# Page gathers spread between rotations, bias sums and a memory copy issued earlier, and a decoder's attention items in another order

## The chip, the cores and the metric

The kernel runs on one core of a Trainium2 chip, in float32. The metric is the device time of one execution in microseconds. Three runs of the kernel before gave 590.39, 592.55 and 594.27 us; the median is 592.55 us.

## The reference, cut to what matters

One layer of a hybrid decoder runs over 512 prompt tokens and over 8 decoding sequences of 4 tokens each, the latter with 1024 past positions in pages of 128. All projections come from one product x @ w_in. The change touches the decoding part (`mla_attend`, `nsa_attend`) and the compression of keys (`compress`):

```python
def compress(kv, w):
    bias = w['cmp_b1'] + jnp.einsum('pkd,kpde->ke', w['cmp_pos_emb'], w1)
    hid = bias[None, None, :, None, :]
    for r in range(ratio):
        proj = jnp.einsum('bcpkgd,kpde->bckge', ch, w1c[:, r])
        hid = hid + proj[:, r:r + nc]
    return jnp.einsum('bckge,ked->bckgd', jax.nn.silu(hid), w['cmp_w2'])

def mla_attend(q_lat, q_rope, q_pos, kv_row, k_pos):
    s = jnp.einsum('bthc,bkc->bhtk', q_lat, ckv) + jnp.einsum('bthr,bkr->bhtk', q_rope, krope)
    p = masked_softmax(s.astype(jnp.float32) * MLA_SCALE, k_pos[None, :] <= q_pos[:, None])
    return jnp.einsum('bhtk,bkc->bthc', p.astype(ckv.dtype), ckv)

def nsa_attend(q, q_rot, q_pos, gates, kv_c, cmp_end, imp_map, gather_sel, win_kv, win_pos):
...
    o = g[:, :, 0] * o_cmp + g[:, :, 1] * o_sel + g[:, :, 2] * o_win
```

Of the three branches of `nsa_attend`, `o_cmp` reads the compressed blocks, whose weights choose the blocks that `o_sel` reads; `o_win` reads the last 512 positions. The updated window buffer `s_win` is one of the outputs: the old buffer moved on by 4 tokens, with the new rows behind.

## The kernel before, in words

`plan()` (L183) writes one list of steps; every engine walks the same list and does its own part of each step, so an engine's order is the list's order. Semaphores join the engines. SP issues all big transfers in an order written out by hand (L713 to L831), with a wait before each that says which buffer has come free.

The stages, in the order of time: the six column blocks of w_in are multiplied one after the other (`proj` steps, blocks B_MLA, B_Q, B_CMPSEL, B_WINGATE, B_ZNSA, B_ZMLA, each for four prompt tiles and the 32 decoding tokens). POOL rotates queries and keys (`rope`, L1911) when ACT has copied a product out; two products later PE transposes the result (`post`). Woven into these, the compressed keys are made: `bias` (L1748 on VectorE: the sum of the position embeddings times cmp_w1, in two products and two reductions, then a small matmul and an addition), then `hid`, `hexp`, `hsilu`, `cmpout` for four groups of past pages and, last, for the prompt (`chunks`). Then come the prompt's attention units (`pscore`, `pnorm`, `pturn`, `pvalue`, numbered 0 to 51), and woven into units 18 to 35 the decoding part; at the end the output product with w_o and the layer norm.

Rotary keys of the past are fetched by 16 indirect DMAs that POOL issues one behind the other in `gather_krope` (L1969), at the step `("hid", 2, 0)`.

Decoding goes by six items (ITEMS, L164): latent attention, selected blocks and sliding window, each for two groups of four sequences. An item is `score` (matmul against the pages in SBUF), `min`, `exp`, `norm`, `probs` (transposes), `pv` (matmul against the pages' values), and for some `oturn`. Pages lie in seven slots of 8 KB per partition (0 to 4 in `ring`, 5 and 6 in `wring`, 7 in `w1h`). LOADS (L356) says for each block of pages its slot and whose `pv` must have ended before SP may load it. A latent or selected block is one sequence's 8 pages, fetched by 8 DMAs whose addresses are page numbers; SP first reads these from `ptab` into registers, 32 of them for four sequences (`numbers`, L670). A block of the window covers two sequences, takes 2 DMAs and needs no page numbers.

The diff touches the functions printed here.

Of the kernel before, what the change touches and what calls it, by code (L numbers as in the profile page):

```python
# [42 lines left out]
GB = 4  # L43
# [120 lines left out]
ITEMS = [("mla", 0), ("mla", 1), ("sel", 0), ("win", 0), ("sel", 1), ("win", 1)]  # L164
# [18 lines left out]
def plan():  # L183
# [21 lines left out]
    for now, _ in products[:first]:  # L205
        steps += now

    cmp = [([("bias",)], .5)]
    for n, t in enumerate(CMP_ORDER):
# [3 lines left out]
        if n == 2:  # L213
# [3 lines left out]
                chunks(1, 1)]  # L217
    cmp.append(([("cmpout", CMP_ORDER[-1])], 1))
    gates = len(products) - 2 * PT - 1
    steps += weave(products[first:gates], cmp + [([], 6)])  # L220
# [30 lines left out]
    for n, x in enumerate(ITEMS):  # L251
# [5 lines left out]
        if last and last[0] != "sel":  # L257
            body.insert(3, ([("oturn", "sel" if last[0] == "win" else "mla", last[1])], 1))
        g = {("mla", 1): 0, ("win", 0): 1}.get(x)
# [3 lines left out]
        if x == ("sel", 0):  # L263
# [61 lines left out]
def o_uses(kind, *a):  # L325
    if kind == "pvalue":
        i, unit, x = UNITS[a[0]]
        return int(spare_bank(i, unit) and x == 0)
    return int(kind in ("cmpout", "zpre") or (kind == "pv" and a[0] != "win"))
# [9 lines left out]
def build(nc, io):  # L339
# [34 lines left out]
    with ExitStack() as ctx:  # L374
# [108 lines left out]
        olatT = take(SR)  # L483
        qm = take(H * QH)
# [36 lines left out]
        impr, impm, dropb = take(SEL_TILES), take(SEL_TILES), take(SEL_TILES)  # L521
# [27 lines left out]
        sel_read = sem("sel_read")  # L549
# [106 lines left out]
        def _(sp):  # L656
# [39 lines left out]
            def load_slot(what, k, after, held=None):  # L696
# [7 lines left out]
                elif after and after[0] == "sel":  # L704
                    sp.wait_ge(sel_read, after[1] + 1)
                elif after:
                    wait_full(sp, O, O.at("pv", *(("sel", after[1]) if after[0] == "win" else after)))
# [57 lines left out]

            sp.wait_ge(gate_done, NT)
# [8 lines left out]

            held = [numbers(b) for b in range(GB)]
            for t in range(NT):
# [32 lines left out]
            wait_full(sp, O, O.at("pv", "sel", NG - 1))  # L810
# [22 lines left out]
        def _(pe):  # L833
# [211 lines left out]
            def weigh(kind, g):  # L1045
# [4 lines left out]
                u = O.at("pv", "sel" if kind == "win" else kind, g)  # L1050
                out = bank_of(O, u) if kind == "win" else claim(O, u)
# [5 lines left out]
                pe.matmul(out[:, 0:P], PTs[0:NS_TOK, pages, :], new, start=(kind != "win"), stop=False)  # L1057
                if kind == "sel":

                    for b in range(GB):  # L1060
                        pe.matmul(out[b * RB:(b + 1) * RB, 0:P], PcT[:, 1, b * RB:(b + 1) * RB],
                                  vc[:, g * GB + b, :], start=False, stop=False)

                for k in range(pages):
                    for b in range(GB):
                        last = k == pages - 1
# [1028 lines left out]
```

## Time and profile before

| | |
|---|---|
| median of three runs | 592.55 us |
| profiled execution | 591.65 us |
| its span, first to last instruction | 589.7 us |
| busy: PE / DVE / ACT / POOL | 491.9 / 258.0 / 153.6 / 135.1 us |
| granted TensorE clock, mean | 0.911 |

The profiled execution is 1.95 us longer than its span. Busy PE time includes matmuls whose ends are modelled, and it is longer where the granted clock is at the lower of its two levels (0.5, which is 1.2 GHz, against 1.0, which is 2.4 GHz).

### The profile page before, as it was taken

The page shows a single profiled execution, that of the slowest core. Times are in us where ns is not written, and L with a number is a line of the kernel's source. Part 1 is how long each engine was busy: PE and PEld are TensorE (multiplying, and loading weights), DVE is VectorE, ACT ScalarE, POOL GpSimd, SP SyncE. Part 2 cuts the span into 40 slices and gives each one's busy share as a digit, 9 for nine tenths or more (in the row PEclk, how much of TensorE's full clock was granted, in tenths as well). Part 3 has the DMA queues.
Part 4 walks back from the last instruction along what each step waited for, and adds up shares of the span by engine and source line. Part 5 has one row for each costly group of instructions (what it writes and reads, how often), then busy time and mean ns, then how long its engine had stood idle before and what let it go on. Part 6 is the DMA issues. An engine that isn't in the chain of part 4 may idle for free. (4 is left out here: it accounts for less than half of the span.)

```text
span 589.7 us, 8838 instructions
## 1 busy us (share of the span) xinstructions
PE 491.9 (83%) x2940; PEld 285.0 (48%) x2940; DVE 258.0 (44%) x673; ACT 153.6 (26%) x431; POOL 135.1 (23%) x222
## 2 busy tenths in 40 slices
PE   6969949999449999799969738468889998999894
PEld 3434436647338554444644525244545665554341
DVE  0041151330302557776966535355425755344415
ACT  0070001211001303433522423133254534233000
POOL 0033532235452111322222111011033432311000
PEclk9979969999859899899959979699889997999898
DMA  8974402442611905000132375864006201002101
GB/s 281 288 246 142 144 1 88 134 144 74 196 53 38 351 6 144 1 2 1 36 110 90 101 252 219 293 190 170 1 1 238 93 1 46 1 1 72 71 0 72
DMA packets 49159, 64.72 MB, mean 110 GB/s; under 512 B 10362, under 2 KB 39546, under 8 KB 49018
## 3 DMA queue, kind: packets, MB, share of 16 engines
q1 hardware_dynamic: 48218, 63.10, 32.3%
q0 software_dynamic: 512, 1.05, 0.7%
q8 instruction: 23, 0.38, 0.3%
q14 instruction: 22, 0.18, 0.1%
q10 hardware_dynamic: 384, 0.01, 0.0%
HBM read 59.89 MB, written 8.41 MB: 116 GB/s over the span
## 5 line engine op out<-in xcount | busy, mean ns | idle before, releaser
L1417 ACT ACTIVATE wring<-wring,small 128x128 f32<-128x128 f32 (+3 forms) x96 | 53.3, 555 | 111.1 <-DVE small L1604 110.6
L888 PE MATMUL psum<-wring,bufA 128*128 128x512 f32 (+1 forms) x192 | 73.6, 538 | 0.0
L1604 DVE CUSTOM_DVE_ANT_0 wring<-psum,const 128x128 f32<-128x128 f32 (+3 forms) x96 | 43.4, 483 | 40.6 <-PE psum L1098 30.8
L870 PE MATMUL psum<-bufA,wring 128*128 128x512 f32 x128 | 60.2, 621 | 0.1
L1314 PE MATMUL psum<-ring,zsil 128*128 128x512 f32 x128 | 58.2, 612 | 0.0
L1950 POOL TENSOR_SCALAR wring<-wring,small,gate 128x128 f32<-128x128 f32 (+3 forms) x32 | 24.3, 760 | 125.6 <-DVE small L1722 124.8
L888 PEld LDWEIGHTS psum<-wring,bufA 128*128 128x128 f32 x192 | 36.7, 194 | 31.4 <-issue 28.4
L843 PE MATMUL psum<-const,wring 128*128 128x128 f32 x248 | 38.7, 287 | 2.4 <-ACT mid L1425 2.4
L843 PEld LDWEIGHTS psum<-const,wring 128*128 128x128 f32 x248 | 28.6, 145 | 22.7 <-issue 17.3
L1314 PEld LDWEIGHTS psum<-ring,zsil 128*128 128x128 f32 x128 | 24.4, 195 | 29.8 <-issue 29.8
L870 PEld LDWEIGHTS psum<-bufA,wring 128*128 128x128 f32 x128 | 24.5, 198 | 28.3 <-issue 28.2
L963 PE MATMUL psum<-ring,w1h 128*128 128x256 f32 x128 | 33.8, 424 | 0.3 <-DVE small L1764 0.3
L1783 DVE RECIPROCAL rtmp<-rtmp 128x512 f32<-128x512 f32 (+1 forms) x10 | 33.5, 3350 | 0.3
L1947 POOL TENSOR_SCALAR wring<-wring,small 128x512 f32<-128x512 f32 (+3 forms) x16 | 19.0, 1187 | 60.4 <-DVE small L1722 60.2
L854 PE MATMUL psum<-wring,bufA 128*128 128x416 f32 x64 | 27.3, 575 | 4.6 <-DMA wring<-in_w_in 4.6
L963 PEld LDWEIGHTS psum<-ring,w1h 128*128 128x128 f32 x128 | 26.9, 215 | 5.4 <-issue 0.7
L843 PE MATMUL psum<-const,bufA 128*128 128x128 f32 (+4 forms) x90 | 15.6, 307 | 15.9 <-ACT mid L1425 7.6
L1966 POOL TENSOR_TENSOR zsil<-zsil,rtmp 128x512 f32<-128x512 f32 (+1 forms) x10 | 12.7, 1265 | 70.3 <-DVE rtmp L1783 70.3
L1014 PE MATMUL psum<-ring,bufA 128*32 128x512 f32 x56 | 15.2, 889 | 16.0 <-DMA ring<-in_sel_pages 8.6
L1144 PE MATMUL psum<-mid,kv 128*64 128x128 f32 x320 | 25.0, 287 | 2.4 <-ACT mid L1425 2.3
L1888 DVE SCALAR_TENSOR_TENSOR bufA<-bufA,psum 128x512 f32<-128x512 f32 x8 | 5.5, 687 | 43.5 <-PE psum L1314 43.5
L1095 PE MATMUL psum<-wring,ring 96*128 96x512 f32 (+3 forms) x64 | 22.0, 468 | 0.2 <-DVE ring L1855 0.2
(234 smaller groups left out, 725.1 us busy)
## 6 DMA issues: line engine op xcount, KB each, us to landing
ring<-in_cmp_pages SPq DMA_DIRECT2D x64, 128.0 KB, 2.3
wring<-in_w_in SPq DMA_DIRECT2D x3, 2048.0 KB, 9.0
ring<-in_sel_pages SPq DMA_DIRECT2D x48, 128.0 KB, 2.3
ring<-in_mla_pages SPq DMA_DIRECT2D x40, 128.0 KB, 2.9
ring<-in_w_om SPq DMA_DIRECT2D x1, 4096.0 KB, 14.2
out_s_win<-in_state_win_kv SPq DMA_DIRECT2D x1, 4064.0 KB
ring<-in_win_pages SPq DMA_DIRECT2D x6, 512.0 KB, 5.8
bufA<-in_x_t SPq DMA_DIRECT2D x8, 272.0 KB, 5.0
```

The costliest lines, as they stand in the source:

```text
L843: return pe.transpose(out, in_, ident[0:in_.shape[0], 0:in_.shape[0]])
L854: ins = pe.matmul(bank[:, 0:w], xT[:, c, t * P:(t + 1) * P], wr[:, 0, c, 0:w], start=(c == 0), stop=(c == KC - 1))
L870: ins = pe.matmul(bank, wr[:, b % 2, k, c * P:(c + 1) * P], xT[:, k, 0:SEQ], start=(k == 0), stop=(k == KC - 1))
L888: ins = pe.matmul(bank[:, 0:w], xT[:, c, t * P:(t + 1) * P], wr[:, b % 2, c, 0:w], start=(c == 0), stop=(c == KC - 1))
L963: ins = pe.matmul(out, w1[:, k, c, :, :].rearrange("p r e -> p (r e)"), chunks, start=(c == 0), stop=(c == 7))
L1095: ins = pe.matmul(bank[:, 0:keys], QT[:, i % 2, h, :], KT[:, h, 0:keys], start=True, stop=True)
L1144: ins = pe.matmul(bank[g * HD:(g + 1) * HD, x * P:(x + 1) * P], v, PTp[:, n % 2, at:at + P], start=(kind == "pmla" and x == 0 and j == 0), ...
L1314: ins = pe.matmul(bank, zT[:, c, ORDER[n] * P:(ORDER[n] + 1) * P], wo[:, c, half * 512:(half + 1) * 512], start=(c == 0), stop=(c == KC - 1))
L1417: ins = act.activation(p, p, ACT.Exp, bias=nmp[:, n % 4, g:g + 1], scale=-1.0, accum_out=lp[:, n % 4, g:g + 1])
L1604: dve.tensor_tensor_reduce(out, src, mask, -scale, CLAMP, ALU.add, ALU.min, least).then_inc(pool.free[u % pool.n], 1)
L1783: dve.reciprocal(e, e).then_inc(z_recip, 1)
L1950: ins = pool.tensor_scalar(p, p, c, gate3[:, i, at:at + 1], ALU.mult, ALU.mult)
```

## The change

Six things are edited.

- The 16 gathers become 16 steps `("krope", at)`. Four stand in each group of compression steps from the second on, between the products; each issues one gather.
- The sums of the bias become a step `bsum` of their own, which stands behind the seventh product (between the first and the second tile of B_Q). The step `bias` keeps the matmul and the addition.
- ITEMS puts both window items before the selected ones. The compressed values now go into the window's product, `pv` of the window and of the selected item have a PSUM use each, and VectorE keeps the window's rows in `orow_win` and adds the selected ones to them. The mask `dropb` is kept per group. The four `vup` steps come earlier, `kup` stays with the last item.
- LOADS is rewritten: the window's four blocks wait for the first latent item and take slots 2, 3, 0, 4; the first group's selected blocks wait for the second latent item (slots 5, 6, 1, 7); the second group's wait for the window items (slots 2, 3, 0, 4).
- On SP, the DRAM copy of the window buffer is issued before the gates' rows. Directly behind the last latent blocks now stand the window loads, the first group's page numbers, its selected blocks, the second group's page numbers and its selected blocks; the 25 stores of new rows, which stood ahead of the selected loads, stand behind all of them.
- `qlat` on PE waits for the copy `qhT` alone (`qh_turned`) instead of the whole `qhead` step; the first latent score waits for that.

```diff
-ITEMS = [("mla", 0), ("mla", 1), ("sel", 0), ("win", 0), ("sel", 1), ("win", 1)]
+ITEMS = [("mla", 0), ("mla", 1), ("win", 0), ("win", 1), ("sel", 0), ("sel", 1)]
...
+    products[NT + 1:NT + 1] = [([("bsum",)], 0)]
...
+        if n:
+            for j in range(4):
+                cmp.insert(len(cmp) - 8 + 2 * j, ([("krope", 4 * (n - 1) + j)], 0))
...
-        g = {("mla", 1): 0, ("win", 0): 1}.get(x)
+        g = {("mla", 1): 0, ("win", 1): 1}.get(x)
...
-        if x == ("sel", 1):
+        if x == ("win", 1):
             body += [([("vup", t)], .9) for t in range(PT)]
...
-             (("sel", 0, 0), 4, ("mla", 0)), (("sel", 0, 1), 2, ("mla", 0)), (("sel", 0, 2), 3, ("mla", 0)),
-             (("sel", 0, 3), 0, ("mla", 0)), (("win", 0, 0), 1, ("mla", 1)), (("win", 0, 1), 7, ("mla", 1)),
-             (("sel", 1, 0), 5, ("mla", 1)), (("sel", 1, 1), 6, ("mla", 1)), (("sel", 1, 2), 4, ("sel", 0)),
-             (("sel", 1, 3), 2, ("sel", 0)), (("win", 1, 0), 3, ("sel", 0)), (("win", 1, 1), 0, ("sel", 0))]
+             (("win", 0, 0), 2, ("mla", 0)), (("win", 0, 1), 3, ("mla", 0)), (("win", 1, 0), 0, ("mla", 0)),
+             (("win", 1, 1), 4, ("mla", 0)), (("sel", 0, 0), 5, ("mla", 1)), (("sel", 0, 1), 6, ("mla", 1)),
+             (("sel", 0, 2), 1, ("mla", 1)), (("sel", 0, 3), 7, ("mla", 1)), (("sel", 1, 0), 2, ("win", 0)),
+             (("sel", 1, 1), 3, ("win", 0)), (("sel", 1, 2), 0, ("win", 1)), (("sel", 1, 3), 4, ("win", 1))]
...
+            sp.dma_start(io["s_win"][0, :, 0:WIN - DEC_T].rearrange("b t k g d -> b (t k g d)"),
+                         io["state_win_kv"][0, :, DEC_T:].rearrange("b t k g d -> b (t k g d)")).then_inc(win_copy, 16)
             sp.wait_ge(gate_done, NT)
...
+            for x in LOADS[8:12]:
+                load_slot(*x)
             held = [numbers(b) for b in range(GB)]
+            for x in LOADS[12:16]:
+                load_slot(*x, held)
+            held = [numbers(GB + b) for b in range(GB)]
+            for x in LOADS[16:]:
+                load_slot(*x, held)
             for t in range(NT):
...
-            for x in LOADS[8:12]:
-                load_slot(*x, held)
-            sp.dma_start(io["s_win"][0, :, 0:WIN - DEC_T].rearrange("b t k g d -> b (t k g d)"),
-                         io["state_win_kv"][0, :, DEC_T:].rearrange("b t k g d -> b (t k g d)")).then_inc(win_copy, 16)
-            held = [numbers(GB + b) for b in range(GB)]
-            for x in LOADS[12:]:
-                load_slot(*x, held)
...
-                if kind == "sel":
+                if kind == "win":

                     for b in range(GB):
...
-                    wait_copied(pe, T, T.at("qhead"))
+                    pe.wait_ge(qh_turned, 1)
                     u = A.at("qlat")
...
+                        wait_copied(pe, T, T.at("qhead"))
-                    if step == ("score", "sel", 0):
+                    if step == ("score", "win", 0):
                         pe.wait_ge(bd_ready, 1)
...
-                if kind == "bias":
+                if kind == "bsum":
                     dve.wait_ge(pos_in, 16)
                     dve.wait_ge(wsmall_in, 16 * 10)
...
                     ins.then_inc(bias_sum, 1)
+                elif kind == "bias":
                     dve.wait_ge(const_in, 16)
...
-                    ok(dve.memset(qbd, 0.0))
-                    dve.tensor_copy(qhT, bank[0:NOPE, :])
+                    dve.memset(qbd, 0.0)
+                    dve.tensor_copy(qhT, bank[0:NOPE, :]).then_inc(qh_turned, 1)
+                    dve.wait_ge(qh_turned, 1)
...
-                    u = O.at("pv", "sel", a[1])
-                    dve.tensor_copy(orow, arrive(O, u)[:, 0:P]).then_inc(O.free[u % O.n], 1)
+                    u = O.at(*step)
+                    dve.tensor_copy(orow_win[:, a[1], :], arrive(O, u)[:, 0:P]).then_inc(O.free[u % O.n], 1)
+                elif kind == "pv" and a[0] == "sel":
+                    u = O.at(*step)
+                    dve.tensor_tensor(orow, arrive(O, u)[:, 0:P], orow_win[:, a[1], :], ALU.add).then_inc(
+                        O.free[u % O.n], 1)
...
-            def gather_krope():
-
-                pool.wait_ge(rope_pages_in, 16 * DEC_B)
...
+            def gather_krope(at):
+
+                if at == 0:
+                    pool.wait_ge(rope_pages_in, 16 * DEC_B)
...
+                g, k = divmod(at, PAGES)
+                pool.indirect_dma_start(
+                    out=krp[:, g, k * P:(k + 1) * P], out_offset=None,
+                    in_=io["krope_pages"].rearrange("n r p -> (n r) p"),
+                    in_offset=bass.IndirectOffsetOnAxis(ap=ropeidx[:, at:at + 1], axis=0)).then_inc(k_land[g], 16)
...
-                if step == ("hid", CMP_ORDER[2], 0):
-                    gather_krope()
+                if step[0] == "krope":
+                    gather_krope(step[1])
```

## Rows read from the trace of the kernel before

**Rows 1.** The waits: engine, line, releaser, us in total, times, longest.
```profile
PE psum L843 <- POOL kv L1925: 16.8, 1, 16.8
...
PE psum L1167 <- DVE mid L1758: 8.3, 1, 8.3
```

**Rows 2.** The timeline (start, length, engine, line, operation): the bias sums and `hid`.
```profile
75.54 2.15 DVE L1755 TENSOR_TENSOR mid<-w1h,mid 128x512 f32<-128x512 f32 x2
...
80.98 1.87 DVE L1758 TENSOR_REDUCE mid<-mid 128x64 f32<-128x1024 f32 x1
...
83.86 6.35 PE L963 MATMUL psum<-ring,w1h 128*128 128x256 f32 x16 [0.31 <-DVE small L1764]
...
103.97 3.72 PE L963 MATMUL psum<-ring,w1h 128*128 128x256 f32 x16
```

**Rows 3.** The timeline of DVE between the first and second tile of B_Q.
```profile
51.37 0.29 DVE L1549 COPY krT<-psum 32x128 f32<-32x128 f32 x1
...
58.28 0.19 DVE L1549 COPY krT<-psum 32x32 f32<-32x32 f32 x1
```

**Rows 4.** The timeline around the gathers.
```profile
146.11 7.71 PE L888 MATMUL psum<-wring,bufA 128*128 128x280 f32 x32
...
150.35 0.20 ACT L1395 ACTIVATE gate<-psum 128x24 f32<-128x24 f32 x1
...
154.41 0.95 POOL L1980 DMA_INDIRECT mid<-in_krope_pages,ropeidx  x1 [5.88 <-issue]
...
168.91 0.32 POOL L1920 TENSOR_TENSOR rtmp<-kv,const 128x64 f32<-128x64 f32 x1
...
170.65 0.69 PE L843 MATMUL psum<-const,kv 128*128 128x128 f32 x2 [16.83 <-POOL kv L1925]
...
171.13 5.31 PE L963 MATMUL psum<-ring,w1h 128*128 128x256 f32 x16
```

**Rows 5.** Windows: busy us (instructions) of PE, PEld, DVE, ACT, POOL; clock, DMA share, GB/s.
```profile
164.10:166.20 2.10, 0.00 (x0) 0.00 (x0) 0.00 (x0) 0.00 (x0) 0.01 (x1) 0.50 0.12 31
...
304.00:308.00 4.00, 4.00 (x22) 2.26 (x23) 2.61 (x10) 2.51 (x6) 0.00 (x0) 0.50 0.01 2
```

**Rows 6.** The timeline around the latent queries.
```profile
298.41 0.42 DVE L1791 COPY bufA<-psum 64x256 f32<-64x256 f32 x1
...
300.73 2.98 PE L1191 MATMUL psum<-bufA,w1h 64*128 64x32 f32 x13 [3.67 <-DVE bufA L1798]
```

**Rows 7.** The timeline of SP's issues; a merged row reaches from its first to its last.
```profile
291.43 8.07 SPq L693 DMA_DIRECT2D wring<-in_mla_pages  x16
...
332.27 16.73 SPq L693 DMA_DIRECT2D ring<-in_sel_pages  x32
349.05 0.83 SPq L800 DMA_DIRECT2D out_s_win<-in_state_win_kv  x1
368.36 0.83 SPq L711 DMA_DIRECT2D ring<-in_win_pages  x2
```

**Rows 8.** Transfers: times issued, KB each, median us from issue to landing.
```profile
ring<-in_sel_pages SPq DMA_DIRECT2D x48, 128.0 KB, 2.3
...
ring<-in_win_pages SPq DMA_DIRECT2D x6, 512.0 KB, 5.8
```

**Rows 9.** The timeline of PE in the decoding stage.
```profile
351.62 3.64 PE L1014 MATMUL psum<-ring,bufA 128*32 128x512 f32 x16 [8.64 <-DMA ring<-in_sel_pages]
...
378.05 1.07 PE L1014 MATMUL psum<-ring,bufA 128*32 128x512 f32 x2 [7.34 <-issue]
...
396.70 1.07 PE L1014 MATMUL psum<-wring,bufA 128*32 128x512 f32 x2 [0.76 <-DMA ring<-in_sel_pages]
...
400.41 2.22 PE L1098 MATMUL psum<-selKT,qrT 64*128 64x512 f32 x4
...
416.64 1.13 PE L1098 MATMUL psum<-winKT,qrT 64*128 64x512 f32 x4
...
445.50 1.08 PE L1067 MATMUL psum<-ring,w1h 128*32 128x128 f32 x32
```

More of the change, by code:

```diff
@@ L204, in plan @@
     first = NT + 3
-    for now, _ in products[:first]:
+    products[NT + 1:NT + 1] = [([("bsum",)], 0)]
+    for now, _ in products[:first + 1]:
         steps += now
@@ L217, in plan @@
                 chunks(1, 1)]
+        if n:
+            for j in range(4):
+                cmp.insert(len(cmp) - 8 + 2 * j, ([("krope", 4 * (n - 1) + j)], 0))
     cmp.append(([("cmpout", CMP_ORDER[-1])], 1))
     gates = len(products) - 2 * PT - 1
-    steps += weave(products[first:gates], cmp + [([], 6)])
+    steps += weave(products[first + 1:gates], cmp + [([], 6)])
     def slot(m):
@@ L256, in plan @@
         body += [([("exp", *x)], 1.5), ([("norm", *x)], 1.5)]
-        if last and last[0] != "sel":
-            body.insert(3, ([("oturn", "sel" if last[0] == "win" else "mla", last[1])], 1))
-        g = {("mla", 1): 0, ("win", 0): 1}.get(x)
+        if last and last[0] != "win":
+            body.insert(3, ([("oturn", *last)], 1))
+        g = {("mla", 1): 0, ("win", 1): 1}.get(x)
         if g is not None:
@@ L328, in o_uses @@
         return int(spare_bank(i, unit) and x == 0)
-    return int(kind in ("cmpout", "zpre") or (kind == "pv" and a[0] != "win"))
+    return int(kind in ("cmpout", "zpre", "pv"))
 def v_uses(kind, *a):
@@ L483, in build @@
         olatT = take(SR)
+        orow_win = qrope.rearrange("p (g n) -> p g n", g=NG)
         qm = take(H * QH)
@@ L520, in build @@
         grow = take(6).rearrange("p (b g) -> p b g", b=3)
-        impr, impm, dropb = take(SEL_TILES), take(SEL_TILES), take(SEL_TILES)
+        impr, impm = take(SEL_TILES), take(SEL_TILES)
+        dropb = [take(SEL_TILES) for _ in range(NG)]
         selc = take(2)
@@ L703, in load_slot @@
                     wait_full(sp, A, A.at("proj", after[1], NT - 1))
-                elif after and after[0] == "sel":
-                    sp.wait_ge(sel_read, after[1] + 1)
                 elif after:
-                    wait_full(sp, O, O.at("pv", *(("sel", after[1]) if after[0] == "win" else after)))
+                    wait_full(sp, O, O.at("pv", *after))
                 kind, g, b = what
@@ L1049, in weigh @@
                     wait_copied(pe, T, T.at("probs", kind, g, j // 2, j=j % 2))
-                u = O.at("pv", "sel" if kind == "win" else kind, g)
-                out = bank_of(O, u) if kind == "win" else claim(O, u)
+                u = O.at("pv", kind, g)
+                out = claim(O, u)[:, 0:P]
                 if kind == "mla":
@@ L1056, in weigh @@
                     new = kv3[0:NS_TOK, ST, col + G * HD:col + KVW]
-                pe.matmul(out[:, 0:P], PTs[0:NS_TOK, pages, :], new, start=(kind != "win"), stop=False)
-                if kind == "sel":
+                pe.matmul(out, PTs[0:NS_TOK, pages, :], new, start=True, stop=False)
+                if kind == "win":
                     for b in range(GB):
-                        pe.matmul(out[b * RB:(b + 1) * RB, 0:P], PcT[:, 1, b * RB:(b + 1) * RB],
-                                  vc[:, g * GB + b, :], start=False, stop=False)
+                        pe.matmul(out[b * RB:(b + 1) * RB, :], PcT[:, 1, b * RB:(b + 1) * RB], vc[:, g * GB + b, :],
+                                  start=False, stop=False)
                 for k in range(pages):
                     for b in range(GB):
-                        last = k == pages - 1
-                        ins = pe.matmul(out[b * RB:(b + 1) * RB, 0:P], PTs[:, k, b * RB:(b + 1) * RB],
-                                        pages_of(kind, g, b)[:, k, P:2 * P], start=False, stop=last and kind != "sel")
-                ins.then_inc(sel_read if kind == "sel" else O.full[u % O.n], 1)
+                        ins = pe.matmul(out[b * RB:(b + 1) * RB, :], PTs[:, k, b * RB:(b + 1) * RB],
+                                        pages_of(kind, g, b)[:, k, P:2 * P], start=False, stop=(k == pages - 1))
+                ins.then_inc(O.full[u % O.n], 1)
             def scores(n):
@@ L1669, in nsa_out, with drop_block @@
                 ins.then_inc(T.free[u % T.n], 1)
-            def drop_block():
+            def drop_block(g):
                 mids = slice(1, SEL_TILES - 2)
@@ L1807, in _ @@
                 elif kind == "norm":
-                    if step == ("norm", "sel", 0):
+                    if step == ("norm", "win", 0):
                         dve.wait_ge(grow_in, 16)
@@ L1843, in _ @@
                     wait_copied(dve, A, A.at("imp1", a[0]))
-                    drop_block()
+                    drop_block(a[0])
                 elif kind == "onsa":
```

27 lines of the change are left out of this document (10 added, 17 removed).

## The prediction

> **What bounds the kernel now.** I read the waits first, then the timeline around the longest of them, then the queue of SP. PE is busy for most of the span, and its busy stretches follow one another by the list of steps; so a wait of PE that goes away brings everything behind it forward, until another wait takes its place. Five waits are touched. PE waits 16.8 us for a rotation on POOL and 8.3 us for the bias sums [rows 1]; 3.67 us for the latent queries [rows 6]; 8.64 and 7.34 us for pages in the decoding stage [rows 9]. The first three are waits for an engine's order. The last two are waits for SP: it is one queue, and in it a page number costs time before any transfer is issued.
>
> **Bias sums.** DVE begins them at 75.54 and ends at 82.85, 7.3 us [rows 2]. PE has nothing else by its list, starts `hid` at 83.86 and needs 6.27 us for it (the next product begins at 90.13), where the same work takes 3.72 at 103.97 [rows 2]: the granted clock had fallen to its lower level behind the wait. In the new place DVE has ended its evictions at 51.66 and is idle until PE's next transposes, some 6.3 us later; the sums would last until 59.0, and the last of three small evictions behind them (0.5 us together) until 59.5, where it ended at 58.47 before [rows 3]. PE's next transposes claim that PSUM bank: 1.0 us lost. At `bias` a small matmul and an addition remain, some 1.4 us: `hid` runs from 76.9 to 80.6 instead of to 90.1. **Gain 9.5 us**, lost cover counted. If POOL's rotations beside the sums slow them by as much as those of rows 2 differ (2.15 against less), it is 8.5; nothing here makes it more than 10.5.
>
> **Gathers.** All 16 stand on POOL ahead of the rotation of the second-last B_CMPSEL product and of all of B_WINGATE. PE ends the second B_WINGATE product at 153.82 and resumes at 170.65; `hid` then takes 5.14 us at the lower clock [rows 4] instead of 3.72 [rows 2]. With the gathers spread, that rotation can begin when ACT has ended at 150.55 and takes 1.7 us (from 168.91 to 170.6) [rows 4]: ready at 152.3, 1.5 us before PE wants it. The next has two gathers ahead of it, 2 x 1.25 us (0.95 and the 0.30 between two), and PE wants it only after a `hid` and a product, 8 us later. `hid` would end at 153.82 + 0.45 + 3.72 = 158.0 instead of at 176.3. **Gain 18.3 us.** Below: one gather waited 5.88 us [rows 4]; if one does so again ahead of a rotation, up to 5 us are lost. Above: nothing, the wait can't be less than none. What is late next? By the list, two `hid`, two products and their transposes stand between (an estimate of 14 us) until the compressed rows that return from DRAM are wanted, and SP's issue of them moves by the 9.5 us of the first term; I estimate 7 us of slack, and more than 20 for the z weights, the next load.
>
> There is a rule against this part. In the trace a gather that waited 2.09 us did so while DVE had no instruction at all [rows 5]. The Trainium skill (SBUF — State Buffer, "A bandwidth-pool intuition that's wrong (but worth ruling out)") says that a DMA issued by GpSimd whose descriptors must be written beside a VectorE copy takes about 3100 ns instead of 620; spread gathers meet more such copies. By it 2.5 us come on to each gather that meets one, and the sum would lose up to 3.5 us at the pair ahead of the second rotation. The row speaks for another cause of these waits, so I leave it out of the sum.
>
> **Latent queries.** `qhT` is copied by 298.83; PE starts at 300.73 [rows 6]. **Gain 1.9 us.** The clock is at the lower level from here to 311 (the window of 304 to 308 has 0.50 with PE fully busy) [rows 5]; if the shorter wait kept it up, some 10 us of work would take 5.5, so the bound above is 6.4. The wait remains and its matmuls are tiny, so I take 1.9.
>
> **Decoding: SP's chain.** Before, SP was free at 299.50 and waited for the first latent `pv` until 332.27 [rows 7]. The page numbers and 25 stores stood in that time, at no cost. Now only windows may be loaded there, and they wait for the same `pv`; numbers and pages follow one by one. The steps, on the clock of before: eight window DMAs, 4 x 0.83 = 3.3 us; 32 page numbers, 18.5 us (from 349.88 to 368.36); 32 page DMAs 16.7; again 18.5; again 16.7 [rows 7]; landing 2.3 [rows 8]. 332.27 + 3.3 + 18.5 + 16.7 + 18.5 + 16.7 + 2.3 = **408.3**, when the second group's selected pages are there. PE started that score at 396.70 [rows 9], 11.6 us sooner.
>
> Would PE be there by then? It loses the waits of 8.64, 7.34 and 0.76 us: the window's 4 MB at 332.27 have 11 us before PE wants the first of them, and one block's DMA lands in 5.8 [rows 8, 9]; the first group's selected pages land at 372.8, and PE, with the units between, wants them at about 382 by my estimate. The work from 400.41 to 416.64, 16.2 us of units, `vup` and window items [rows 9], now stands ahead of that score. 396.70 - 16.7 + 16.2 = 396.2, and sooner by what of the first selected item now follows; so PE waits 12 us or more, once, instead of twice. Behind the score, 445.50 + 1.08 - 396.70 = 49.9 us of before lose the 16.2 and gain about 2 (the last item has eight pages where it had four: a second 1.08, and four more transposes) [rows 9]: 35.7. The last `pv` ends at 444.0 instead of 446.6. **Gain 2.6 us.** If PE needs 5 us more there (behind the score ACT has all `kup` copies ahead of the last `exp`), it is a loss of 2; if SP's chain binds less than I think, the gain is at most 2.6 + 12 = 14.6, which is a rival.
>
> **At nothing.** The memory copy: 0.83 us on SP [rows 7], ahead of the gates' rows and the last latent blocks; SP then waits long for the last product anyway (until 291.43) [rows 7], and the copy has that time for itself; without that cover its transfer, at most the 29 us between 349.05 and 378.05, would delay both. Before, it lay ahead of the window loads of 368.36. The 25 stores are wanted by nobody, and the norm's weights and w_o are issued behind waits that come later still. The separate masks and the kept window rows cost two additions of DVE beside PE's work.
>
> **The sum.** 9.5 + 18.3 + 1.9 + 2.6 = 32.3 us. 591.65 - 32.3 = 559.4 for the profiled execution; the median is 0.9 us above that one: **560 us**.
>
> **The rivals.**
> *SP's chain doesn't bind.* If number reads and issues overlapped, or PE came later than I think, 12 us more: 548. Against it: 18.5 us passed between two issues with no wait in between that was still open [rows 7]. Chance 0.12.
> *The gains are given back.* PE, 28 us earlier, meets a load of SP that did not move with it (the rows from DRAM or the z weights), and half of the gathers' gain goes: 560 + 9 = 569. For it: SP's numbers ahead of those loads. Against it: the slacks above. Chance 0.12.
> *Gathers wait each time.* A gather that waits 5.88 us holds POOL for 5.88 + 0.95 + 0.30 = 7.1 us [rows 4], 114 us for 16, where the work that they are spread over takes PE an estimated 70 to 90 us (ten gathers over some 59 us from the second B_CMPSEL product to the last of B_WINGATE, the rest over three products with their silu on POOL). With POOL's own rotations it would end some 40 us late, and PE with it: 600, slower than before. It decides from a mean wait of about 4.5 us on; at fewer the cost vanishes between the products. For it: a long wait did occur. Against: seven gathers had gone out back to back before it, and here at most two stand together. Chance 0.04. The rule of the Trainium skill (same page and section) points the same way, with 2.5 us a gather.
>
> **How the numbers follow.** The forecast has the remaining 0.72, and its own range is 552 to 569 (the bounds of the terms: 6 us below, with the clock and the first bound of the decoding; 9 above). With the rivals on either side the range is 547 to 572. About 1% is what can be told from no change here: faster 0.93, same 0.03, slower 0.04.
>
> **What would show it.** Right: no PE wait for POOL's rotation near 144, no 8 us wait ahead of `bias`, gathers in ones and twos with no long gaps, and in the decoding stage one wait of PE, 12 to 20 us, at the second selected score, with SP's two runs of 32 page DMAs and some 18 us before each. Wrong: two or more page waits, or none; a rotation that comes behind a waiting gather; the lower clock in other places; a wait for the rows returned from DRAM.

## The result, and the profile after

The kernel after takes **554.37 us** (median of four runs, 553.57 to 555.21), the kernel before in the same series 591.47; the ratio is 0.9366, with a 95% interval of 0.9327 to 0.9405. The forecast was 560 us, with a range of 547 to 572. The profiled execution of after took 554.15 us (span 552.3, mean granted clock 0.937, where before it was 0.911).

The waits of PE in the kernel after, longest first (engine, line, releaser; us in total, times, longest):

```profile
PE psum L1019 <- DMA ring<-in_sel_pages: 17.5, 1, 17.5
PE psum L848 <- ACT mid L1430: 10.3, 12, 2.8
PE psum L859 <- DMA wring<-in_w_in: 4.9, 1, 4.9
```

The two longest of [rows 1] are gone. One wait for pages is left. The many small waits for ACT were 10.2 us in the kernel before.

The timeline of after, from the first evictions of the second block to the latent queries; it answers to [rows 2 to 4] and [rows 6]:

```profile
50.08 0.29 DVE L1554 COPY krT<-psum 32x128 f32<-32x128 f32 x1
50.40 1.83 DVE L1760 TENSOR_TENSOR mid<-w1h,mid 128x512 f32<-128x512 f32 x2
...
58.63 0.63 PE L848 MATMUL psum<-const,comp 128*128 128x128 f32 x4 [1.42 <-DVE krT L1554]
...
75.74 3.72 PE L968 MATMUL psum<-ring,w1h 128*128 128x256 f32 x16 [0.68 <-DVE small L1770]
...
79.39 1.95 PE L898 MATMUL psum<-wring,bufA 128*32 128x128 f32 x64
...
139.89 0.32 POOL L1931 TENSOR_TENSOR rtmp<-kv,const 128x64 f32<-128x64 f32 x1 [3.88 <-ACT gate L1400]
...
140.80 3.35 DVE L1604 RECIPROCAL w1h<-w1h 64x512 f32<-64x512 f32 x1
...
142.02 0.98 POOL L1990 DMA_INDIRECT mid<-in_krope_pages,ropeidx  x1 [0.27 <-POOL kv L1936]
...
142.92 0.38 PE L848 MATMUL psum<-const,kv 128*128 128x128 f32 x2
...
143.14 3.62 PE L968 MATMUL psum<-ring,w1h 128*128 128x256 f32 x16
...
145.18 0.95 POOL L1990 DMA_INDIRECT mid<-in_krope_pages,ropeidx  x1 [2.18 <-issue]
...
268.88 2.98 PE L1195 MATMUL psum<-bufA,w1h 64*128 64x32 f32 x13 [2.12 <-DVE bufA L1797]
```

The sums begin at 50.40, at once behind the last eviction, and cost PE a wait of 1.42 us there. The first `hid` takes 3.72 us where it took 6.35. The rotation starts at 139.89, as soon as ACT has copied the product out, and PE's transposes follow at 142.92 with no wait, where they had 16.83 us. A gather goes out behind the rotation and not ahead of it.

The decoding stage of after, the queue of SP (a merged row reaches from its first to its last) and then PE; it answers to [rows 7] and [rows 9]:

```profile
299.92 3.85 SPq L715 DMA_DIRECT2D ring<-in_win_pages  x8
322.10 8.87 SPq L699 DMA_DIRECT2D wring<-in_sel_pages  x16
...
335.62 4.40 SPq L699 DMA_DIRECT2D w1h<-in_sel_pages  x8
358.15 16.29 SPq L699 DMA_DIRECT2D ring<-in_sel_pages  x32
...
377.27 3.64 PE L1019 MATMUL psum<-ring,bufA 128*32 128x512 f32 x16 [17.54 <-DMA ring<-in_sel_pages]
...
410.23 1.95 PE L1071 MATMUL psum<-ring,w1h 128*32 128x128 f32 x64
```

From 340.02 to 358.15 SP issues nothing: 18.1 us for 32 page numbers, 0.57 us each. From SP's first window DMA to the score 77.35 us pass; the prediction had 76.0.

Where the time went, by stretches between the same steps (us, from the traces; the third column is a second profile of the unchanged kernel before, told of below):

| stretch, up to | before | before again | after | after less before | predicted |
|---|---|---|---|---|---|
| last eviction ahead of the sums (51.37, 49.71, 50.08) | 51.37 | 49.71 | 50.08 | -1.29 | 0 |
| product behind the first `hid` (90.14, 88.17, 79.39) | 38.77 | 38.46 | 29.31 | -9.46 | -9.5 |
| product behind the late `hid` (176.27, 174.17, 146.59) | 86.13 | 86.00 | 67.20 | -18.93 | -18.3 |
| latent queries (300.73, 300.20, 268.88) | 124.46 | 126.03 | 122.29 | -2.17 | -1.9 |
| first latent `pv` (329.72, 328.38, 297.52) | 28.99 | 28.18 | 28.64 | -0.35 | 0 |
| end of the last `pv` (446.58, 440.73, 412.18) | 116.86 | 112.35 | 114.66 | -2.20 | -2.6 |
| end of the span | 143.12 | 143.17 | 140.12 | -3.00 | 0 |

In the stretches of the four terms 32.8 us are gone, against 32.3 forecast. The first two terms are plain there. The last two are not: two profiles of the unchanged kernel differ by 1.57 us in the stretch of the latent queries and by 4.51 in that of the decoding. The profiled pair has 4.6 us more, most of them in two stretches that the prediction put at nothing.

### The profile page after: what moved, and what is told of

Same layout as the page of the kernel before. It is cut to its first block and busy times, and to the rows that moved or that the text cites. A ratio compares the mean times of both kernels' runs of the same rounds, so it can differ in the third digit from the quotient of the medians.

```text
span 552.3 us, 8832 instructions
## 1 busy us (share of the span) xinstructions
PE 480.9 (87%) x2940; PEld 280.4 (51%) x2940; DVE 257.8 (47%) x675; ACT 153.7 (28%) x431; POOL 136.0 (25%) x222
## 5 line engine op out<-in xcount | busy, mean ns | idle before, releaser
L1609 DVE CUSTOM_DVE_ANT_0 wring<-psum,const 128x128 f32<-128x128 f32 (+3 forms) x96 | 43.3, 483 | 39.8 <-PE psum L1102 30.2
L1319 PE MATMUL psum<-ring,zsil 128*128 128x512 f32 x128 | 56.5, 597 | 0.0
L848 PE MATMUL psum<-const,wring 128*128 128x128 f32 x248 | 40.0, 294 | 0.4 <-ACT mid L1430 0.4
L848 PEld LDWEIGHTS psum<-const,wring 128*128 128x128 f32 x248 | 29.4, 149 | 21.3 <-issue 18.8
L968 PE MATMUL psum<-ring,w1h 128*128 128x256 f32 x128 | 29.5, 383 | 0.7 <-DVE small L1770 0.7
L1019 PE MATMUL psum<-ring,bufA 128*32 128x512 f32 x56 | 13.5, 858 | 17.5 <-DMA ring<-in_sel_pages 17.5
L1148 PE MATMUL psum<-mid,kv 128*64 128x128 f32 x320 | 26.6, 299 | 2.4 <-ACT mid L1430 2.3
L848 PE MATMUL psum<-const,bufA 128*128 128x128 f32 (+4 forms) x90 | 14.3, 288 | 14.8 <-ACT mid L1430 9.6
L968 PEld LDWEIGHTS psum<-ring,w1h 128*128 128x128 f32 x128 | 23.8, 190 | 4.5 <-DVE small L1770 0.8
L1148 PEld LDWEIGHTS psum<-mid,kv 128*64 128x64 f32 x320 | 18.2, 145 | 8.7 <-issue 5.0
```

The source lines that it names most:

```text
L848: return pe.transpose(out, in_, ident[0:in_.shape[0], 0:in_.shape[0]])
L968: ins = pe.matmul(out, w1[:, k, c, :, :].rearrange("p r e -> p (r e)"), chunks, start=(c == 0), stop=(c == 7))
L1148: ins = pe.matmul(bank[g * HD:(g + 1) * HD, x * P:(x + 1) * P], v, PTp[:, n % 2, at:at + P], start=(kind == "pmla" and x == 0 and j == 0), ...
L1319: ins = pe.matmul(bank, zT[:, c, ORDER[n] * P:(ORDER[n] + 1) * P], wo[:, c, half * 512:(half + 1) * 512], start=(c == 0), stop=(c == KC - 1))
L1609: dve.tensor_tensor_reduce(out, src, mask, -scale, CLAMP, ALU.add, ALU.min, least).then_inc(pool.free[u % pool.n], 1)
```

## The experiments

Each kernel was timed in three rounds beside the kernel before (medians of that: 590.07 us in the series of e1 to e4, 591.11 in that of e5 to e8, 590.06 in that of e9 to e12), but for e9, which has one run. Where a kernel is compared with before, the gain is worked out from the ratio; where it is compared with after, it is the difference of two medians from different series. By the ratios these last come out up to 2 us otherwise (10.9 us for e10, 22.3 for e11, 9.2 for e5, 12.9 for e12), each give or take 3 to 4 us.

| kernel | median us | ratio to before, 95% |
|---|---|---|
| e1_bsum | 585.31 | 0.9899 (0.9862 to 0.9936) |
| e2_krope | 568.53 | 0.9624 (0.959 to 0.9657) |
| e3_qlat | 588.52 | 0.9964 (0.9929 to 0.9999) |
| e4_order | 586.84 | 0.9939 (0.9919 to 0.9959) |
| e5_6_early | 544.20 | 0.9211 (0.9168 to 0.9253) |
| e6_first_early | 556.39 | 0.9417 (0.9374 to 0.9459) |
| e7_copy_late | 556.18 | 0.9425 (0.9383 to 0.9467) |
| e8_gathers_at_once | 555.59 | 0.9401 (0.9355 to 0.9448) |
| e9_before_again | 585.96 | one run |
| e10_no_bsum | 564.03 | 0.955 (0.9502 to 0.9599) |
| e11_no_krope | 575.62 | 0.9744 (0.9692 to 0.9797) |
| e12_half_twice | 567.02 | 0.9584 (0.9534 to 0.9635) |

**The bias sums, put in alone and taken out alone.** e1 is before with

```diff
+    products[NT + 1:NT + 1] = [([("bsum",)], 0)]
-                if kind == "bias":
+                if kind == "bsum":
...
+                elif kind == "bias":
                     dve.wait_ge(const_in, 16)
```

> The kernel before with one edit: the sums of the bias stand in their new place, all else as before. Theory A (the prediction's term): the wait of 8.3 us ahead of the bias goes and the first hid runs at the upper clock, 1 us is lost at the new place: 9.5 us faster (8.5 to 10.5), ratio about 0.984. Rival: PE, earlier by that, meets a load of SP that did not move, and the gain shows at the first hid but not at the end: 0 to 5 us. In addition, the kernel after had its first evictions of the second block 1.3 us sooner and its last part, from the last pv on, 3.0 us shorter than the kernel before; if these come from the place where the lower clock falls, they should show here or not with no relation to the edit.

Measured: 6.0 us faster (3.8 to 8.2), less than the term. At the next `hid` (92.95 before, 83.23 here) the whole gain was still there. So the same edit was taken out of the kernel after: e10 is after with the lines above turned round.

> The kernel after with the bias sums back in their old place, all else as after. Alone in the kernel before, their move gave 6.0 us (3.8 to 8.2) where 9.5 was expected, while the trace had the 9.5 at the first hid and lost 2.9 us between the first and the last pv. Theory A (the term is right, and the lower clock in the old decoding stage hid some of it): 9.5 us slower than the kernel after, ratio to before about 0.953. Rival: the bias sums are worth no more than 6 us at the end in either surrounding: ratio about 0.947.

Measured: 564.03 us, 9.7 more than after. Its timeline has the old wait and the slow `hid` back:

```profile
82.70 0.56 PE L1170 MATMUL psum<-const,mid 128*64 128x1 f32 x4 [8.26 <-DVE mid L1762]
83.57 5.13 PE L967 MATMUL psum<-ring,w1h 128*128 128x256 f32 x16 [0.31 <-DVE small L1768]
```

So the term of 9.5 us is right, and the rival is out. What e1 lost, its profile lost far behind the edit; the windows under e9 show where.

**The gathers, put in alone, taken out alone, and in one block.** e2 is before with the spread steps:

```diff
+        if n:
+            for j in range(4):
+                cmp.insert(len(cmp) - 8 + 2 * j, ([("krope", 4 * (n - 1) + j)], 0))
...
-                if step == ("hid", CMP_ORDER[2], 0):
-                    gather_krope()
+                if step[0] == "krope":
+                    gather_krope(step[1])
```

> The kernel before with one edit: the 16 gathers are single steps spread over the compression, all else as before. Theory A (the prediction's term): PE's wait of 16.8 us for the rotation goes and the hid behind it takes 3.7 us instead of 5.1: 18.3 us faster, ratio about 0.969. Rival: each gather that meets work of VectorE waits some 2.5 us, and PE meets a wait for POOL elsewhere: less than 13 us faster. Second rival: the gain is there at the end of the projections and is given back later at a load of SP: about 9 us faster.

e11 is after with that undone, the block at its old step:

> The kernel after with the 16 gathers back in one block in their old place, all else as after. Alone in the kernel before, spreading them gave 22.2 us (20.2 to 24.2) where 18.3 was expected. Theory A (the term of 18.3 us is right, the rest is the clock): 18.3 us slower than the kernel after, up to 20 with the lower clock behind the wait, ratio to before about 0.968. Rival: the wait brings down the clock in later places too, so that it costs 22 us in either surrounding: ratio about 0.975.

Measured: 22.2 us faster alone (20.2 to 24.2), and 21.3 slower than after when taken out. Both are above 18.3: in e11 it was the rival that came, 22 us in either surrounding. The timeline of PE in e11:

```profile
135.94 7.71 PE L890 MATMUL psum<-wring,bufA 128*128 128x280 f32 x32
160.51 0.69 PE L845 MATMUL psum<-const,kv 128*128 128x128 f32 x2 [16.85 <-POOL kv L1933]
160.99 6.39 PE L965 MATMUL psum<-ring,w1h 128*128 128x256 f32 x16
167.21 2.99 PE L890 MATMUL psum<-wring,bufA 128*128 128x280 f32 x12
```

From the start of the gate product to the next product 31.27 us pass; in the kernel after they are 11.22 (135.37 to 146.59). That is 20.05 us at this place alone: the wait of 16.85 and a `hid` of 6.2 us, where the one of [rows 4] was through in 5.1 and the one of after in 3.5. The other 1.3 us between the two spans lie in no one place.

Is it the spreading that counts? e8 is after with all 16 issued at the first of the new steps:

```diff
-                if step[0] == "krope":
-                    gather_krope(step[1])
+                if step == ("krope", 0):
+                    for at in range(NG * PAGES):
+                        gather_krope(at)
```

> The kernel after with one edit: all 16 gathers are issued at the first of their steps, beside the B_CMPSEL products, instead of spread. Theory A (what counts is that no rotation which PE waits for stands behind the whole of them): the gathers take some 28 us at a stretch, as in the kernel before, and now hold up the rotations of B_CMPSEL there: 5 to 17 us slower than the kernel after, by how early POOL is. Rival B (the order among the steps counts, not the spreading): 0 to 1 us.

Measured: 555.59 us, not to be told from after. POOL's timeline in e8:

```profile
107.77 1.17 POOL L1990 DMA_INDIRECT mid<-in_krope_pages,ropeidx  x1 [0.57 <-POOL ropeidx L1984]
...
115.49 0.94 POOL L1990 DMA_INDIRECT mid<-in_krope_pages,ropeidx  x1 [0.30 <-issue]
119.89 0.95 POOL L1990 DMA_INDIRECT mid<-in_krope_pages,ropeidx  x1 [3.45 <-issue]
...
131.77 0.94 POOL L1990 DMA_INDIRECT mid<-in_krope_pages,ropeidx  x1 [2.05 <-issue]
132.74 0.33 POOL L1931 TENSOR_TENSOR rtmp<-kv,const 128x64 f32<-128x64 f32 x1
```

The block holds POOL for 25 us here too, and the rotations of these products queue behind it. But PE's longest wait between 100 and 200 us in e8 is 0.6 us: these rotations are wanted so much later that POOL has caught up. My theory A fell. What the change removed is a block at a place where the next rotation was due at once; spreading was one way, an earlier place does as well.

**The latent queries alone.** e3 is before with

```diff
-                    wait_copied(pe, T, T.at("qhead"))
+                    pe.wait_ge(qh_turned, 1)
                     u = A.at("qlat")
...
-                    ok(dve.memset(qbd, 0.0))
-                    dve.tensor_copy(qhT, bank[0:NOPE, :])
+                    dve.memset(qbd, 0.0)
+                    dve.tensor_copy(qhT, bank[0:NOPE, :]).then_inc(qh_turned, 1)
```

> The kernel before with one edit: the latent queries wait for the copy of the queries alone. Theory A (the prediction's term): 1.9 us sooner at the latent queries and no change of the clock: ratio about 0.997, which three rounds may not tell from no change, so the trace decides: the wait of 3.67 us becomes 1.8. Upper bound: the shorter wait keeps the clock at its upper level: 6.4 us. Rival: SP's chain of page numbers and loads starts at the end of the first latent pv and moves with it, so the gain stays in either case; if it is lost, something that did not move, the latent pages or the compressed values, holds PE in the decoding stage: 0.

```profile
297.05 2.98 PE L1192 MATMUL psum<-bufA,w1h 64*128 64x32 f32 x13 [1.80 <-DVE bufA L1793]
```

Measured: 2.1 us faster (0.1 to 4.2). PE's wait is 1.80 us instead of 3.67, and from the last decoding product of the projections to the queries 9.58 us pass instead of 11.45, so 1.87 less; the clock behind it is still the lower one.

**The new order alone.** e4 is before with all of the change's diff but the three edits above: ITEMS, LOADS, SP's order and the copy.

```diff
-ITEMS = [("mla", 0), ("mla", 1), ("sel", 0), ("win", 0), ("sel", 1), ("win", 1)]
+ITEMS = [("mla", 0), ("mla", 1), ("win", 0), ("win", 1), ("sel", 0), ("sel", 1)]
```

> The kernel before with the rest of the change: the new order of items and loads, the page numbers and stores in their new places on SP, the copy of the window buffer sooner; without the other three edits. Theory A (the prediction's term): two page waits become one of 12 to 20 us at the second selected score, 2.6 us faster at the last pv: ratio about 0.996. Theory B: the last part of the kernel after, which was 3.0 us shorter than before, is so because of the new order: 5.6 us, ratio about 0.990. Rival: without the earlier start of everything the old order is better, and this part alone is slower by up to 2 us.

Measured: 3.6 us faster (2.4 to 4.8), which holds the 2.6 of Theory A and not the 5.6 of Theory B. Two page waits became one, of 18.67 us:

```profile
409.16 3.37 PE L1014 MATMUL psum<-ring,bufA 128*32 128x512 f32 x16 [18.67 <-DMA ring<-in_sel_pages]
```

**Page numbers: half of a run taken off the path, half a run put on, and the first run moved.** e5 is after with

```diff
+            held = [numbers(b) for b in range(GB)]
+            later = [numbers(GB + b) for b in range(2)]
             for x in LOADS[8:12]:
                 load_slot(*x)
-            held = [numbers(b) for b in range(GB)]
             for x in LOADS[12:16]:
                 load_slot(*x, held)
-            held = [numbers(GB + b) for b in range(GB)]
-            for x in LOADS[16:]:
-                load_slot(*x, held)
+            for x in LOADS[16:18]:
+                load_slot(*x, later)
+            later += [numbers(GB + b) for b in range(2, GB)]
+            for x in LOADS[18:]:
+                load_slot(*x, later)
```

> The kernel after with one edit: SP reads the first group's 32 page numbers and 16 of the second group's in the 30 us in which it waits for the first latent pv, ahead of the window loads; the second group's other 16 numbers stand between its two halves of loads. Theory A (SP's chain of numbers sets the second selected score): the first group's pages are issued from the end of the second latent pv (321) to 339, half of the second group's to 347, 16 numbers 9 us, the rest from 356 to 365, landed at 367 instead of 377: 10 us faster than the kernel after, ratio to before about 0.92, and PE's wait of 17.5 us becomes about 8. Rival B: the wait is for the pages' transfers or the window's values, not for the numbers: 0 to 2 us. Rival C: PE gains 10 us at the score and meets a later wait (ACT's copies, the z units): half of it.

Measured: **544.20 us**, 10.2 less than after and the fastest kernel of this study. In the profiles 8.2 us are at the score, 50.38 us behind the second latent `pv` (318.87) instead of 58.61. SP and PE in e5:

```profile
321.76 8.70 SPq L699 DMA_DIRECT2D wring<-in_sel_pages  x16
...
334.76 4.61 SPq L699 DMA_DIRECT2D w1h<-in_sel_pages  x8
339.55 27.15 SPq L699 DMA_DIRECT2D ring<-in_sel_pages  x32
...
369.25 3.54 PE L1022 MATMUL psum<-ring,bufA 128*32 128x512 f32 x16 [7.70 <-DMA ring<-in_sel_pages]
```

PE's wait is 7.70 us where it was 17.54. The numbers no longer set it: the window item that frees the last two of the eight slots (0 to 7) ends at 358.44, 16 page DMAs and their landing follow, and 369.25 is there.

e6 moves only the first group's numbers ahead of the window loads:

```diff
+            held = [numbers(b) for b in range(GB)]
             for x in LOADS[8:12]:
                 load_slot(*x)
-            held = [numbers(b) for b in range(GB)]
```

> The kernel after with one edit: the first group's 32 page numbers are read ahead of the window loads. Theory A: in the kernel after they were hidden already, since SP issued the first selected page at 322.1 and the second latent pv, for which it would wait otherwise, ended at 321.0: 1 us faster, not to be told from the kernel after. Rival: the prediction's arithmetic, by which each run of numbers stands on the path for its full 18 us: 18 us faster, or as much of it as PE's wait of 17.5 us allows.

```profile
378.48 3.64 PE L1019 MATMUL psum<-ring,bufA 128*32 128x512 f32 x16 [17.32 <-DMA ring<-in_sel_pages]
```

Measured: 556.39 us, no gain. The score stands 58.37 us behind the second latent `pv` (320.11 to 378.48), in the kernel after 58.61. The first run of numbers was hidden: its end (322.1) and that of the `pv` that SP would wait for otherwise (321.0) lie 1.1 us apart.

e12 adds to the kernel after, ahead of the second run:

```diff
+            for b in range(2):
+                numbers(GB + b)
             held = [numbers(GB + b) for b in range(GB)]
```

> The kernel after with one thing added: SP reads the first 16 of the second group's 32 page numbers twice. Theory A (SP's chain of page numbers sets the second selected score, at about 0.57 us each): 9.1 us more at that score and at the end, PE's wait of 17.5 us becomes 26.6, ratio to before about 0.952. Rival: the reads go beside transfers that PE waits for anyway: 0 to 3 us.

```profile
368.49 3.43 SPq L699 DMA_DIRECT2D ring<-in_sel_pages  x7
...
388.10 3.64 PE L1021 MATMUL psum<-ring,bufA 128*32 128x512 f32 x16 [26.52 <-DMA ring<-in_sel_pages]
```

The wait grew by 8.98 us, which is 16 times 0.56: in the kernel after the second run stands on the path one for one. The median is 12.6 us above that of after. The profiled span is 13.6 us longer (565.9 against 552.3): beside the 8.98 us it has 1.5 at the start and 2.6 in the last part, which the reads don't touch.

**The copy of the window buffer.** e7 is after with the copy issued later:

```diff
-            sp.dma_start(io["s_win"][0, :, 0:WIN - DEC_T].rearrange("b t k g d -> b (t k g d)"),
...
             for x in LOADS[12:16]:
                 load_slot(*x, held)
+            sp.dma_start(io["s_win"][0, :, 0:WIN - DEC_T].rearrange("b t k g d -> b (t k g d)"),
+                         io["state_win_kv"][0, :, DEC_T:].rearrange("b t k g d -> b (t k g d)")).then_inc(win_copy, 16)
             held = [numbers(GB + b) for b in range(GB)]
```

> The kernel after with one edit: the copy of the window buffer is issued between the first group's selected pages and the second group's page numbers. Theory A (the copy was moved for nothing): 0.8 us of SP on the path and the transfer beside the numbers: 0 to 2 us slower than the kernel after. Rival: the copy of 4 MB holds up the pages of the second group behind it, as the gates' rows were held up by 21.8 us in the kernel after: 5 us slower or more.

Measured: 556.18 us, no difference that can be told. The transfer of the gates' rows, the small DMA that is issued next to the copy (KB, then median us from issue to landing), in the kernel after:

```profile
gate_rows<-gate SPq DMA_DIRECT2D x1, 3.0 KB, 22.2
```

and in e7:

```profile
gate_rows<-gate SPq DMA_DIRECT2D x1, 3.0 KB, 2.2
```

The 4 MB ahead of it hold 3 KB up for 20 us. SP has that time, since its next load waits until 261. The Trainium skill (DMA: Bandwidth & Descriptors, "Queues, rings and completion order") says that each DMA engine takes its descriptors in ring order and that a completion is signalled only when all earlier writes of that engine are done; 22.2 against 2.2 us agrees.

**The kernel before, once more** (e9, unedited).

> The kernel before once more, unedited, for a second profile of it. Open question: the kernel after had its first evictions of the second block 1.3 us sooner, and its last part, from the last pv to the end, was 2.1 us shorter by the start of that pv; beside that the stretch from the first to the last pv took 115.4 us in the kernel before and 118.3, 120.6 and 117.4 in the three kernels with the old order of items and one other edit. Theory A (where the lower clock falls differs from run to run): this profile differs from the first one by some us in the same stretches, with other places of the lower clock: the first to the last pv 115 to 121 us, the last part 142.5 to 144.6. Theory B (the edits did it): the stretches are those of the first profile, within 0.3 us.

Measured: 585.96 us, span 583.9, 5.8 us shorter than the first profile of the same kernel. Of these, 4.5 us lie in the decoding stage. So Theory B is out, and the profiles do differ as Theory A has it, but by more than its range: from the first latent `pv` to the start of the last one 110.85 us pass, not 115 to 121. The windows from the first latent `pv` to the end of the last one, and from there to the end of the span (us; busy us and instructions of PE, PEld, DVE, ACT, POOL; mean granted clock, DMA share, GB/s), first of before:

```profile
329.72:446.58 116.86, 84.94 (x820) 51.17 (x820) 52.46 (x170) 39.49 (x97) 18.24 (x25) 0.87 0.44 154
446.58:589.70 143.12, 124.57 (x654) 71.20 (x653) 66.48 (x169) 40.45 (x105) 27.50 (x32) 0.94 0.17 61
```

of e9:

```profile
328.38:440.73 112.35, 82.36 (x820) 49.83 (x820) 52.53 (x170) 39.52 (x97) 18.23 (x25) 0.91 0.47 160
440.73:583.90 143.17, 124.61 (x653) 71.28 (x653) 66.55 (x169) 40.46 (x105) 27.49 (x32) 0.95 0.17 61
```

of e2, which has the same decoding stage:

```profile
308.30:430.35 122.05, 90.97 (x820) 54.94 (x820) 52.73 (x170) 39.63 (x97) 18.23 (x25) 0.83 0.43 147
430.35:571.60 141.25, 121.87 (x654) 69.79 (x653) 66.46 (x169) 40.46 (x105) 27.51 (x32) 0.98 0.17 62
```

and of after:

```profile
297.52:412.18 114.66, 84.20 (x820) 52.36 (x820) 51.85 (x172) 39.57 (x97) 18.48 (x25) 0.85 0.41 133
412.18:552.30 140.12, 121.82 (x654) 69.58 (x653) 66.54 (x169) 40.45 (x105) 27.50 (x32) 0.97 0.17 63
```

Read the first rows like this. The 820 matmuls of the stage are the same everywhere, but PE is busy with them for 82.36 us at a mean clock of 0.91 and for 90.97 at 0.83. The stage less PE's busy time is 31.9, 30.0, 31.1 and, after, 30.5 us. With the old order the stage took 112.4 to 122.1 us in five profiles (e1 119.8, e3 118.9), and 8.6 of these 9.7 us are PE's busy time at another clock. That is where e1's profile lost part of its gain: its clock there was 0.84. With the new order, and the second run of page numbers as in after, seven profiles had 113.9 to 115.1 us. The last part of the span is 143.1 us in three profiles of the old order (clock 0.94 to 0.95) and 141.3 in the other two (0.98); with the new order it is 140.1 to 140.2 us in six, 141.8 in two (0.96) and 142.8 in e12 (0.94).

## Why the prediction held, step by step

- **Bias sums, 9.5 us.** Right: 9.46 in the traces, 9.7 by e10. PE's loss at the new place, put at 1.0, shows as a wait of 1.42.
- **Gathers, 18.3 us.** Right in mechanism, too small in size. The traces of before and after have 18.93; e11 has 20.05 at the same place, and the medians 21.3. I had priced the `hid` behind the wait by the 1.4 us that one profile showed; the lower clock there took 1.7 to 2.8 us, and the rest lies in no one place. The weighing of one long wait ahead of a rotation was not needed: in the kernel after, only the eighth and the sixteenth gather paused (2.18 and 2.08 us), and no rotation was late for PE.
- **Latent queries, 1.9 us.** Right, 1.87 in e3; the clock did stay at its lower level.
- **Decoding, SP's chain, 2.6 us.** The forecast wait of 12 to 20 us came, 17.54, in its place, and e5 and e12 show that the second run of page numbers sets it. Two things in the step were not as I put them. The first run did not lie on the chain, as I had added it: it ended 1.1 us behind the `pv` that would have held SP to nearly the same moment (e6), so the chain's sum was right by that coincidence. And the 2.6 us were to come from less waiting of PE. PE's time without work in the stage was 31.9 us before and 30.5 after (30.0 to 31.9 in five profiles of the old order, 30.2 to 33.0 in seven of the new); 16.7 us of page waits became 17.5. So the forecast of 2.6 us came near (2.20 in the profiled pair) by luck. What the order gained by itself (3.6 us in e4) has no place in the traces that is clear of noise: e4's stage of 114.31 us lies within the 112.4 to 122.1 of the old order. On the average of five profiles against seven the stage takes 118.0 us against 114.6, and PE is busy in it for 87.3 (82.4 to 91.0) against 83.4 (80.9 to 84.4), while the rest is no shorter (30.7, 31.3). The mean granted clock of the stage is 0.86 on the average of either group (0.83 to 0.91, 0.85 to 0.88), so nothing shows that one long wait brings the clock down for less time than two shorter ones. Worked out from the records of the clock and of PE, more of the time at the lower level falls where PE has no work: 13.4 to 15.5 us with the new order, 7.5 to 12.4 with the old. That would shorten the busy time; it was not tried by itself.
- **At nothing.** The copy (e7) and the gates' rows cost nothing that could be told, and PE waits for no mask and no kept window row; the stores (the trace of before has 22 of them, not 25) were not tried by themselves.
- **The sum.** 32.3 us were forecast and 37.1 measured. The parts, 9.7 (e10) and 21.3 (e11) as differences of medians and 2.1 (e3) and 3.6 (e4) by the ratios, make 36.7, each good to 1 to 4 us. So some 3 of the 5 us that were missing belong to the gathers' term, and perhaps 1 to the order's. Of the gathers' 3 us, 1.4 are PE's slower `hid` behind the wait (2.8 us longer in e11, where I had put 1.4). In the profiled pair the excess shows elsewhere: at the start (the same code ended there between 49.71 and 51.56 in the profiles of this study) and in the last part, where 2.75 of the 3.00 us are PE's busy time (124.57 and 121.82) at another mean clock (0.94 and 0.97). That comes and goes in both orders: e2, with the old one, has 121.87, and e12, with the new one, 124.55.

The rivals: *SP's chain doesn't bind* is refuted by e12, *the gains are given back* by the table, in which the gain in each stretch adds to the one before, and *gathers wait each time* by e8. In e8's block VectorE was busy for 5.93 of 24.94 us, and yet 13 of the 15 gathers that follow another came 0.30 or 0.31 us behind it; the long pauses fell on the eighth and the sixteenth, as in the kernel after. The gather at 142.02 took 0.98 us in the kernel after while VectorE was busy throughout, with the reciprocal of 140.80. The rule of the Trainium skill (SBUF — State Buffer, "A bandwidth-pool intuition that's wrong (but worth ruling out)") is for a VectorE copy, beside which a GpSimd DMA takes some 3100 ns. It is not tried here: in after and e8 no gather stands beside a copy longer than 0.41 us, so the copies that the prediction feared were not there.

## What to carry to other kernels

Before spreading a block of work on a side engine, ask when its next result is due: an earlier place for the whole block was worth as much here as the spreading. On a queue that reads addresses into registers, count the reads like transfers, and do them in the time in which the queue waits anyway: moving the 16 that bound the last score took another 8 us there, and 10 in the medians. Whether the old order of items, with its page numbers read ahead, would do as well was not tried. Price a long wait with what the clock takes behind it, and don't judge a stage by one profile: the same 820 matmuls kept PE busy from 82 to 91 us.

## What was not expected of the hardware

- One page number read into a register of SP takes 0.56 to 0.57 us (18.1 us for 32, 8.98 us for 16 more), about as much as the issue of a 128 KB page DMA (0.52 us).
- Indirect gathers paused at the eighth and the sixteenth (2.18 and 2.08 us spread, 3.45 and 2.05 in one block), whatever stood between them; the others followed at 1.25 us in a block. What is full at the eighth, no run here shows. The long pauses at the eighth (5.88 us in before, 3.45 in e8) fell where the DMA engines were busy for 0.80 and 0.85 of the time, the ones of 2.05 to 2.18 us where it was 0.10 to 0.37 (before, e2, e8, after); whether the traffic makes them long was not tried.
- The decoding stage with the old order differed by 9.7 us between profiles with the granted clock; two executions of one kernel differed by 5.7 us (591.65 and 585.96), and the 19 of before in the series of e1 to e4 lie between 586.92 and 593.58.
